# Extra products in TensorE's gaps between the output projection and the first expert

## The chip, the cores and the metric

The kernel runs on one core of a Trainium2 chip. The metric is the device time of one execution in microseconds (us). Three runs of the kernel before took 1212.13, 1212.85 and 1215.75 us, a median of 1212.85.

## What is computed

One layer for 336 tokens (16 meta tokens, 256 of a prompt, 64 of eight samples) of 1024 channels. A retention branch and a convolution branch are merged, projected by `w_out` and normalised. Then each token goes through two of 16 experts. The part that matters here, cut from the reference:

```python
mixed = (sigmoid(m_r) * ret_out + sigmoid(m_c) * conv_out) @ w_out
x = _layernorm(alpha * x + mixed, ln1_g, ln1_b)
logits = (xt @ w_router).astype(float32) + b_router
probs = softmax(logits)                        # best group of four experts,
                                               # then the best two inside it
for e in range(16):
    he = silu(xt @ w_gate[e]) * (xt @ w_up[e])
    y = y + gates[:, e:e + 1] * (he @ w_down[e])
x = _layernorm(alpha * x + y, ln2_g, ln2_b)
```

## The kernel before

Each engine has its own program, written out by hand, and executes it in order. They wait for each other with semaphores. The tokens stand in three tiles t = 0, 1, 2 of 112. There are eight PSUM banks of 128 x 512 f32; each named result ("xt0", "log0") has a bank by a fixed turn, four banks for names of kind F and four for kind P. `room` waits until the result that had the bank before has been read out.

Weight products are split: a weight is rounded to a high part on ScalarE (`split_hi` line 1081, `hi_of` line 1265), the remainder is formed on VectorE (line 1086, line 1690), and TensorE multiplies in the format fp32r. The small products and the transposes are done in plain f32: the router, the positions, the gather by a matrix, and `prompt_state` of the retention stage (line 964).

The stage around the change goes like this.

- TensorE ends the output projection (`t_unit` with WOUT, line 1036). VectorE adds the residual and normalises each tile (lines 1627, 1609 to 1621), and increments `x1_ready` for each. The square root in it is ScalarE's (line 1246).
- For each tile t, TensorE waits for `x1_ready`, transposes the tile in eight pieces of 112 x 128 (`turn`, line 1053), and multiplies the transposed tile by the router's weights (`router`, line 1042). ScalarE copies the transposes out (line 1249); in its program the square root of tile t+1 stands behind the copies of tile t. The router's result log0 uses the bank that the last tile's output projection had, so its first product needs VectorE's line 1627 of tile 2. The transposes of tile 2 need log0's bank again, which VectorE reads out in line 1639, behind `x1_ready` of tile 2.
- VectorE then picks two experts per token in a chain of small operations (lines 1642 to 1663) and sets `chosen_ready`. TensorE counts the tokens ahead of each in its experts by products with a triangular matrix (lines 1059, 1062). VectorE reads this (line 1671) into `most_i`, on which all engines branch, then makes `picks` (line 1677) and the slots (line 1683).
- GpSimd scatters the tokens to `x_slots` in DRAM, six indirect DMAs (line 682), and once all have landed reads the tokens of expert 1 (`xg_tok`, line 686).
- The tokens of expert 0 don't take this way: TensorE gathers them with 24 products by `picks` (line 830). VectorE meanwhile scales y (line 1684), splits two weight units (line 1690), and then forms the low part of the gathered tokens (line 1695). Then the first expert starts (`expert`, line 800). Within it, after six of its twelve weight units, TensorE transposes the tokens of the next expert (`tokens`, line 768 and on), which it waits for by `xg_full`.

The weights come by SyncE's queue into eight slots, each released by VectorE's low part (line 505).

In the trace a plain f32 product shows as two MATMUL records and a transpose or an fp32r product as one; the names x and tab stand for x1 and for the tables, ident among them.

Of the kernel before, what the change touches and what calls it, by code (L numbers as in the profile page):

```python
# [158 lines left out]
def alone(eng, waits_met):  # L159

    eng.sem_inc(waits_met, 1)
# [13 lines left out]
def program(nc, x_prompt, x_sample, state_ret, state_conv, meta_tokens, w_in, b_in, w_ret_o, conv_w, conv_b,  # L175
# [10 lines left out]
    with ctx:  # L186
# [3 lines left out]
        def sb(name, shape, dt=f32):  # L190
            size = 4 * int(np.prod(shape[1:]))
            t = nc.alloc_sbuf_tensor_at(name, shape, dt, offset=base[0])
            base[0] += (size + 31) // 32 * 32
            high[0] = max(high[0], base[0])
            return t

        def sem(name):
            return ctx.enter_context(nc.semaphore(name))


        tab = sb("tab", [128, TBW])
# [123 lines left out]
        bank = [ctx.enter_context(nc.psum_tensor(f"bank{i}", [128, 512], f32)) for i in range(8)]  # L325
        ident = tab[:, TB["ident"][0]:TB["ident"][1]]
# [22 lines left out]
        CONV = Stage(GATE2, ["Fc0", "Fc1", "Fc2", "Fc3"], 2)  # L349
# [30 lines left out]
        evac = [sem(f"evac{i}") for i in range(8)]  # L380
# [51 lines left out]
        def T_view(t, slot):  # L432
            return t[:, slot, :].rearrange("p (k n) -> p k n", k=4)
# [286 lines left out]
        def _(pe):  # L720
# [24 lines left out]
            def t_unit(stage, half, parts, finals, it, wh, wl, xh, xl):  # L745

                for t in range(NT):
                    name = finals[t]
                    if half == 0:
                        room(stage, name, it)  # L750
                    out = bank[stage.bank[name]][0:TT, :]
                    mms = []
                    for k in range(4):
                        kk = 4 * half + k
                        first, last = half == 0 and k == 0, half == 1 and k == 3
                        xs = slice(t * TT, (t + 1) * TT)
                        mms += [(out, xh[:, kk, xs], wh[:, k, :], first, False), (out, xh[:, kk, xs], wl[:, k, :], False, False),
                                (out, xl[:, kk, xs], wh[:, k, :], False, last)]
                    group(stage, name, it, mms)
# [8 lines left out]
            def gathered_path():  # L768
                def tokens(stage, names, q, it, value):

                    pe.wait_ge(xg_full[q], value)
                    for j, name in enumerate(names):
                        b = bank[stage.bank[name]]
                        turn(stage, name, it, [(b[:, i * CAP:(i + 1) * CAP], xg_tok[:, q, (4 * j + i) * 128:(4 * j + i + 1) * 128], CAP) for i in range(4)])

                def half(stage, v, it, wit, name, kh, xh, xl):

                    pe.wait_ge(mlo_ready, U_PAIR.idx(v, wit) + (1 + MLEAD))
                    if kh == 0:
                        room(stage, name, it)  # L780
                    out = bank[stage.bank[name]][0:CAP, :]
                    wh, wl = T_view(mhi, v % MH), T_view(mlo, v % MH)
                    mms = []
                    for k in range(4):
                        kk = 4 * kh + k
                        mms += [(out, xh[:, kk, :], wh[:, k, :], kk == 0, False), (out, xh[:, kk, :], wl[:, k, :], False, False),
                                (out, xl[:, kk, :], wh[:, k, :], False, kk == KT - 1)]
                    group(stage, name, it, mms)

                def h_turn(stage, p, j, it):  # L790

                    pe.wait_ge(evac[stage.bank[f"u{p}{j}"]], stage.used(f"u{p}{j}", it) + 1)
                    alone(pe, waits_met)
                    b = bank[stage.bank[f"ht{p}{j}"]]
                    turn(stage, f"ht{p}{j}", it, [(b[:, i * CAP:(i + 1) * CAP], h_tok[:, (4 * j + i) * 128:(4 * j + i + 1) * 128], CAP) for i in range(4)])

                def evacuated(stage, name, it):
                    pe.wait_ge(evac[stage.bank[name]], stage.used(name, it) + 1)

                def expert(stage, p, it, wit, following):  # L800
                    v = 12 * p
                    xh, xl = xg_hi[:, p], xg_lo[:, p]
                    if p:
                        for j in range(2):
                            evacuated(stage, f"xt0{j}", it)
                    for u, name in ((0, f"g{p}0"), (2, f"u{p}0")):
                        for kh in range(2):
                            half(stage, v + u + kh, it, wit, name, kh, xh, xl)
                    for kh in range(2):
                        half(stage, v + 4 + kh, it, wit, f"g{p}1", kh, xh, xl)  # L810
                    h_turn(stage, p, 0, it)
                    if following:
                        tokens(stage, (f"xt{p}0", f"xt{p}1"), 1 - p, it, wit * 16 + 16)
                    for kh in range(2):
                        half(stage, v + 6 + kh, it, wit, f"u{p}1", kh, xh, xl)
                    for kh in range(2):
                        evacuated(stage, f"ht{p}{kh}", it)
                        for n in range(2):
                            half(stage, v + 8 + 2 * kh + n, it, wit, f"d{p}{n}", kh, hT_hi, hT_lo)
                            if kh == 0 and n == 0:  # L820
                                h_turn(stage, p, 1, it)

                pe.wait_ge(picks_ready, NT)
                for j in range(2):
                    room(FIRST, f"xt{j}", 0)
                    b = bank[FIRST.bank[f"xt{j}"]]
                    for i in range(4):
                        ch = (4 * j + i) * 128
                        for t in range(NT):
                            last = pe.matmul(b[:, i * CAP:(i + 1) * CAP], x1[:, t, ch:ch + 128], picks[:, t, :], start=t == 0, stop=t == NT - 1)  # L830
                    last.then_inc(group_done, 1)
                for j in range(2):
                    evacuated(FIRST, f"xt{j}", 0)
                for it in range(NE // 2 - 1):
                    for p in range(2):
                        if p == 0:

                            pe.wait_ge(turned, it + 1)
                        expert(PAIR, p, it, it, True)
                pe.wait_ge(turned, NE // 2)  # L840
                expert(LAST, 0, 0, NE // 2 - 1, True)
                expert(LAST, 1, 0, NE // 2 - 1, False)
# [18 lines left out]
            for t in (1, 2, 0):  # L861
# [4 lines left out]
                for j in range(2):  # L866
                    n = f"xt{2 * t + j}"
# [5 lines left out]
            for h in range(H):  # L873
# [61 lines left out]
                for t in (2, 1, 0):  # L935
# [5 lines left out]
                    if t == 0:  # L941
# [5 lines left out]
                        for r in range(2):  # L947
                            for p in range(2):
                                for c in range(4):
                                    i = pe.matmul(bank[HEAD.bank[name]][32 * c:32 * c + QC, :], qdiag[:, p, c + 4 * r, :], st[:, c + 4 * r, p, :],  # L950
                                                  start=False, stop=(r == 1 and p == 1), skip_group_check=True)
# [80 lines left out]
            for n in range(2):  # L1032
                for half in range(2):
                    pe.wait_ge(mlo_done, half + 1)
                    split_ready(U_WOUT, 2 * n + half, 0)
                    t_unit(WOUT, half, None, [f"w{n}{t}" for t in range(NT)], 0, T_view(hi, half), T_view(lo, half), m_hi, m_lo)
            def router(t):
                for n in (2 * t, 2 * t + 1):
                    pe.wait_ge(evac[X1T.bank[f"xt{n}"]], X1T.used(f"xt{n}") + 1)
                room(X1T, f"log{t}", 0)  # L1040
                out = bank[X1T.bank[f"log{t}"]]
                group(X1T, f"log{t}", 0, [(out[0:TT, 0:NE], x1T_f[:, k, t * TT:(t + 1) * TT], wr_sb[:, k, :], k == 0, k == KT - 1) for k in range(KT)])
# [5 lines left out]
            for t in range(NT):  # L1048
                pe.wait_ge(x1_ready, t + 1)
                for j in range(2):  # L1050
                    n = f"xt{2 * t + j}"
                    b = bank[X1T.bank[n]]
                    turn(X1T, n, 0, [(b[:, i * TT:(i + 1) * TT], x1[:, t, (4 * j + i) * 128:(4 * j + i + 1) * 128], TT) for i in range(4)])
                router(t)

            pe.wait_ge(chosen_ready, 1)
            room(X1T, "pos", 0)
# [2 lines left out]
            for i in range(NT):  # L1060
                n = NT - i
                last = pe.matmul(out[0:TT, (i + 1) * NE:(NT + 1) * NE].rearrange("p (t e) -> p t e", t=n), ones_t,
                                 gt[:, 7, i, :].unsqueeze(1).to_broadcast([TT, n, NE]), start=False, stop=True, skip_group_check=True)
            last.then_inc(group_done, 1)
            pe.wait_ge(most_ready, 1)
            with pe.If(pe.value_load(most_i[0:1, 0:1], min_val=0, max_val=T) <= CAP):
                gathered_path()
# [756 lines left out]
```

## Time and profile before

| | |
|---|---|
| median of three runs | 1212.85 us |
| the profiled execution's own time | 1213.8 us |
| its span, first to last instruction | 1212.0 us |
| TensorE busy | 1120.5 us (92%) |
| VectorE busy | 955.2 us (79%) |
| ScalarE busy | 637.9 us (53%) |
| mean granted TensorE clock | 0.965 |

A granted clock of 1.00 is 2.4 GHz, 0.50 is 1.2 GHz. The span runs through three long parts: retention and convolution up to about 548 us, the stage described above from there to about 608 us, and the experts up to about 1170 us, with the last normalisation behind. A time such as 573.34 is counted from the span's start. A row of a timeline gives the start, the length of the whole merged group, the engine, the line, the operation, out<-in and the count; in brackets stands the idle time ahead of it and what ended it.

### The profile page before, as it was taken

The page shows a single profiled execution, that of the slowest core. Times are in us where ns is not written, and L with a number is a line of the kernel's source. Part 1 is how long each engine was busy: PE and PEld are TensorE (multiplying, and loading weights), DVE is VectorE, ACT ScalarE, POOL GpSimd, SP SyncE. Part 2 cuts the span into 40 slices and gives each one's busy share as a digit, 9 for nine tenths or more (in the row PEclk, how much of TensorE's full clock was granted, in tenths as well). Part 3 has the DMA queues.
Part 4 walks back from the last instruction along what each step waited for, and adds up shares of the span by engine and source line. Part 5 has one row for each costly group of instructions (what it writes and reads, how often), then busy time and mean ns, then how long its engine had stood idle before and what let it go on. Part 6 is the DMA issues. An engine that isn't in the chain of part 4 may idle for free.

```text
span 1212.0 us, 15132 instructions
## 1 busy us (share of the span) xinstructions
PE 1120.5 (92%) x5829; PEld 873.8 (72%) x5829; DVE 955.2 (79%) x1021; ACT 637.9 (53%) x582; POOL 127.3 (10%) x219
## 2 busy tenths in 40 slices
PE   4999999999999999997799999999999999999960
PEld 4986986987798699985667676767766676776640
DVE  3598898889789885556568888888888888888846
ACT  2432433244243236431267777777777777777730
POOL 3120220220212030000210000000000000000012
PEclk9999999999999999998599999999999999999985
DMA  9663874785486395453399999999999999999924
GB/s 214 204 228 124 278 255 138 245 278 201 152 274 224 124 272 178 139 204 109 108 353 366 377 379 388 374 380 379 380 377 379 382 383 379 380 380 380 384 95 107
DMA packets 171323, 331.85 MB, mean 274 GB/s; under 512 B 8394, under 2 KB 45690, under 8 KB 171232
## 3 DMA queue, kind: packets, MB, share of 16 engines
q1 hardware_dynamic: 150624, 263.95, 62.1%
q0 software_dynamic: 20352, 66.41, 16.6%
q8 instruction: 49, 0.80, 0.3%
q10 hardware_dynamic: 272, 0.47, 0.2%
q14 instruction: 26, 0.21, 0.1%
HBM read 294.88 MB, written 36.63 MB: 274 GB/s over the span
## 4 chain that ended last, share of the span: by engine, by line
PE 78%; DVE 11%; DMA 4%; ACT 3%; issue 2%; POOL 1%; SPq 0%; POOLq 0%; DVEq 0%; ACTq 0%
PE bank L724 74%; PE bank L765 3%; DVE lo L1086 3%; DVE cT L1391 2%; DMA x_in<-in_x_prompt_dram 1%; ACT hi L1081 1%; PE bank L975 1%; DVE st L1535 1%; DMA x_slots<-x,slot 1%; POOL x_slots L682 1%; DMA xg_tok<-x_slots 1%; DMA y_back<-y_slots,slot 1%; ACT hi L1225 1%; DVE o_tok L1497 0%; DVE stats L1489 0%
## 5 line engine op out<-in xcount | busy, mean ns | idle before, releaser
L1690 DVE TENSOR_TENSOR mlo<-mraw,mhi 128x2048 fp32r<-128x2048 f32 x192 | 439.4, 2289 | 78.8 <-ACT mhi L1265 75.5
L1265 ACT ACTIVATE mhi<-mraw 128x2048 fp32r<-128x2048 f32 x192 | 367.4, 1915 | 91.7 <-PE bank L724 85.0
L724 PE MATMUL bank<-mhi,xg_hi 128*96 128x512 f32 x512 | 203.0, 396 | 1.4 <-DVE xg_lo L1695 1.4
L724 PE MATMUL bank<-mhi,xg_lo 128*96 128x512 f32 x512 | 202.7, 396 | 0.0
L724 PE MATMUL bank<-mlo,xg_hi 128*96 128x512 f32 x512 | 201.5, 394 | 0.0
L1081 ACT ACTIVATE hi<-raw 128x2048 fp32r<-128x2048 f32 x47 | 89.9, 1914 | 195.0 <-PE bank L724 167.5
L1086 DVE TENSOR_TENSOR lo<-raw,hi 128x2048 fp32r<-128x2048 f32 x56 | 128.3, 2291 | 78.6 <-ACT hi L1081 43.5
L724 PE MATMUL bank<-xT_hi,hi 128*128 128x336 f32 x512 | 166.0, 324 | 3.1 <-DVE lo L1086 1.7
L724 PE MATMUL bank<-xT_hi,lo 128*128 128x336 f32 x512 | 163.9, 320 | 0.0
L724 PE MATMUL bank<-xT_lo,hi 128*128 128x336 f32 x512 | 163.8, 320 | 0.0
L1391 DVE SCALAR_TENSOR_TENSOR cT<-W,vec,cT 128x336 f32<-128x336 f32 x240 | 118.6, 563 | 0.0
L724 PEld LDWEIGHTS bank<-mhi,xg_hi 128*96 128x96 f32 x512 | 82.9, 162 | 36.2 <-issue 1.7
L724 PEld LDWEIGHTS bank<-mhi,xg_lo 128*96 128x96 f32 x512 | 82.9, 162 | 36.1
L724 PEld LDWEIGHTS bank<-mlo,xg_hi 128*96 128x96 f32 x512 | 83.2, 162 | 35.5
L724 PE MATMUL bank<-mhi,hT_hi 128*96 128x512 f32 x256 | 101.7, 397 | 0.0
L724 PEld LDWEIGHTS bank<-xT_hi,hi 128*128 128x128 f32 x512 | 98.7, 193 | 4.0 <-DVE lo L1086 2.0
L724 PE MATMUL bank<-mhi,hT_lo 128*96 128x512 f32 x256 | 100.8, 394 | 0.0
L724 PE MATMUL bank<-mlo,hT_hi 128*96 128x512 f32 x256 | 100.6, 393 | 0.0
L724 PEld LDWEIGHTS bank<-xT_lo,hi 128*128 128x128 f32 x512 | 98.7, 193 | 0.2
L724 PEld LDWEIGHTS bank<-xT_hi,lo 128*128 128x128 f32 x512 | 98.6, 193 | 0.0
L724 PE MATMUL bank<-hi,xT_lo 128*112 128x512 f32 x144 | 56.9, 395 | 0.0
L697 POOL DMA_DIRECT2D y_slots<-yo x14 | 7.1, 507 | 467.2 <-ACT yo L1294 467.2
(253 smaller groups left out, 1496.6 us busy)
## 6 DMA issues: line engine op xcount, KB each, us to landing
mraw<-in_w_gate_dram SPq DMA_DIRECT2D x64, 1024.0 KB, 11.4
mraw<-in_w_up_dram SPq DMA_DIRECT2D x64, 1024.0 KB, 11.3
mraw<-in_w_down_dram SPq DMA_DIRECT2D x64, 1024.0 KB, 12.0
raw<-in_w_in_dram SPq DMA_DIRECT2D x40, 1024.0 KB, 6.7
st<-in_state_ret_dram POOLq DMA_DIRECT2D x32, 512.0 KB, 5.0
out_dram<-st POOLq DMA_DIRECT2D x32, 512.0 KB, 4.5
raw<-in_w_ret_o_dram SPq DMA_DIRECT2D x8, 1024.0 KB, 5.4
x_slots<-zeros POOLq DMA_DIRECT2D x12, 512.0 KB, 4.2
```

The lines of the kernel that those rows point to most:

```text
L682: pool.indirect_dma_start(x_slots, bass.IndirectOffsetOnAxis(slot[:, k, t:t + 1], 0), x1[:, t, :], None).then_inc(scattered, 16)
L697: pool.dma_start(y_slots[ds((it * 2 + p) * CAP, CAP), :], yo[:, p, :]).then_inc(yo_stored, 16)
L724: i = pe.matmul(out, a, b, start=s, stop=e)
L765: i = pe.transpose(out, in_, ident[0:n, 0:n])
L975: i = pe.matmul(bank[HEAD.bank[f"st{b}{p}"]][:, :], a[rows, b // 4, cols], v[rows, :], start=k == 0, stop=k == 2)
L1081: act.activation(dst[:, hslot, :], src[:, slot, :], ACT.Copy).then_inc(ready, 1)
L1086: dve.tensor_tensor(l[:, u % RH, :], src[:, u % R, :], h[:, u % RH, :].bitcast(f32), ALU.subtract).then_inc(lready, 1)
L1225: act.activation(hi[:, slot, :], raw[:, slot, :], ACT.Copy).then_inc(hi_ready, 1)
L1265: act.activation(mhi[:, v % MH, :], mraw[:, v % MR, :], ACT.Copy).then_inc(mhi_ready, 1)
L1391: ins = dve.scalar_tensor_tensor(out, src, tap, out, ALU.mult, ALU.add)
L1535: dve.scalar_tensor_tensor(st[:, s, p, :], st[:, s, p, :], hs[:, HGAM:HGAM + 1], b[:, :], ALU.mult, ALU.add).then_inc(e, 1)
L1690: dve.tensor_tensor(mlo[:, v % MH, :], mraw[:, v % MR, :], mhi[:, v % MH, :].bitcast(f32), ALU.subtract).then_inc(mlo_ready, 1)
```

## The change

A function `keep_warm(n)` issues n plain f32 products of the 128 x 128 identity by 512 columns of the tables, all into the bank of the convolution's last result c3, which nobody reads again before a later product overwrites it. It is called eight times in TensorE's program: behind the transposes of tile 0, 1 and 2 with 12, 1 and 1; behind the router's products of these tiles with 3, 7 and 12; behind the products for the positions with 3; and behind the gather of the first expert's tokens with 2. No other engine's program is changed, and no semaphore is incremented by the products.

```diff
@@ -829,6 +829,7 @@
                     last.then_inc(group_done, 1)
+                keep_warm(2)
                 for j in range(2):
                     evacuated(FIRST, f"xt{j}", 0)
@@ -1034,7 +1035,14 @@
+            def keep_warm(n):
+
+                pe.wait_ge(evac[CONV.bank["c3"]], CONV.used("c3", 1) + 1)
+                for _ in range(n):
+                    pe.matmul(bank[CONV.bank["c3"]][:, :], ident, tab[:, 128:640], start=True, stop=True)
+
             def router(t):
+                keep_warm((12, 1, 1)[t])
                 for n in (2 * t, 2 * t + 1):
                     pe.wait_ge(evac[X1T.bank[f"xt{n}"]], X1T.used(f"xt{n}") + 1)
@@ -1052,6 +1060,7 @@
                 router(t)
+                keep_warm((3, 7, 12)[t])
 
             pe.wait_ge(chosen_ready, 1)
@@ -1062,6 +1071,7 @@
             last.then_inc(group_done, 1)
+            keep_warm(3)
             pe.wait_ge(most_ready, 1)
```

## Rows read from the trace of the kernel before

**Rows 1.** The page: busy time of the engines; TensorE's granted clock in 40 slices.
```profile
PE 1120.5 (92%) x5829; PEld 873.8 (72%) x5829; DVE 955.2 (79%) x1021; ACT 637.9 (53%) x582; POOL 127.3 (10%) x219
...
PEclk9999999999999999998599999999999999999985
```

**Rows 2.** The chain of waits, 540 to 690 us: start, length, what.
```profile
578.64 0.10 ACT lnmv L1246
...
594.46 0.19 DVE most L1671
...
598.92 5.12 POOL x_slots L682
...
609.29 10.49 DMA x_slots<-x,slot
...
620.38 7.60 DMA xg_tok<-x_slots
```

**Rows 3.** Stretches: length, busy time by engine, TensorE's granted clock, DMA share, GB/s.
```profile
570.00:573.30 3.30, 0.00 (x0) 0.00 (x0) 3.13 (x5) 0.00 (x0) 0.00 (x0) 0.52 0.00 0
573.30:588.00 14.70, 12.72 (x64) 11.93 (x64) 5.44 (x11) 3.55 (x6) 0.55 (x16) 0.50 0.32 111
...
607.96:611.03 3.07, 3.07 (x8) 2.02 (x8) 2.15 (x1) 0.88 (x1) 2.67 (x2) 0.50 1.04 406
611.03:626.30 15.27, 15.27 (x69) 10.61 (x68) 10.47 (x7) 11.28 (x7) 1.51 (x2) 1.00 0.99 340
```

**Rows 4.** TensorE's timeline, 566 to 629 us.
```profile
566.35 1.22 PE L765 MATMUL bank<-tab,x 112*128 112x112 f32 x8 [0.86 <-issue]
573.34 3.14 PE L724 MATMUL bank<-wr_sb,x1T_f 128*112 128x16 f32 x16 [5.78 <-DVE x L1627]
576.32 1.73 PE L765 MATMUL bank<-tab,x 112*128 112x112 f32 x8
...
584.81 3.14 PE L724 MATMUL bank<-wr_sb,x1T_f 128*112 128x16 f32 x16 [0.68 <-issue]
592.68 0.61 PE L1059 MATMUL bank<-gt,tab 112*112 112x48 f32 x2 [4.73 <-DVE gt L1663]
...
595.99 10.53 PE L830 MATMUL bank<-picks,x 112*128 112x96 f32 x48 [1.64 <-DVE picks L1677]
607.96 0.71 PE L724 MATMUL bank<-mhi,xg_hi 128*96 128x512 f32 x1 [1.44 <-DVE xg_lo L1695]
...
628.11 0.85 PE L765 MATMUL bank<-tab,xg_tok 96*128 96x96 f32 x8 [1.50 <-DMA xg_tok<-x_slots]
```

**Rows 5.** TensorE's plain f32 products in the retention stage: groups by form, timeline.
```profile
L724 PE MATMUL bank<-v_tok,kdp 112*128 112x512 f32 x48 | 22.0, 595 | 0.0
...
82.78 0.55 PE L724 MATMUL bank<-qr,kr 128*112 128x112 f32 x4
...
100.94 2.75 PE L724 MATMUL bank<-v_tok,kdp 112*128 112x512 f32 x6
```

**Rows 6.** VectorE's timeline, 572 to 608 us.
```profile
572.51 0.68 DVE L1627 SCALAR_TENSOR_TENSOR x<-x_tok,bank 112x512 f32<-112x512 f32 x1
...
578.76 0.81 DVE L1614 TENSOR_SCALAR x<-x,lnmv 112x1024 f32<-112x1024 f32 x1 [3.41 <-ACT lnmv L1246]
...
582.13 0.26 DVE L1639 TENSOR_TENSOR gt<-bank,br_bc 112x16 f32<-112x16 f32 x2
...
603.07 0.55 DVE L1695 TENSOR_TENSOR xg_lo<-bank,xg_hi 128x384 fp32r<-128x384 f32 x1
607.14 0.56 DVE L1695 TENSOR_TENSOR xg_lo<-bank,xg_hi 128x384 fp32r<-128x384 f32 x1 [3.52 <-ACT xg_hi L1269]
```

**Rows 7.** ScalarE's timeline: copies of the transposes of tile 0, square root of tile 2.
```profile
566.96 1.19 ACT L1249 ACTIVATE x1T_f<-bank 128x448 f32<-128x448 f32 x2 [4.08 <-PE bank L765]
...
578.53 0.19 ACT L1246 ACTIVATE lnmv<-lnmv 112x1 f32<-112x1 f32 x1
```

## The prediction

> **What bounds the kernel now.** I read the page first. TensorE is busy 92% of the span, and its clock is full except in slices 19 and 20 and in the last two [rows 1]. A slice is 30.3 us, so the low clock lies within 545 to 606 us and a little beyond: the stage between the output projection and the experts. The chain of waits shows what sets the time there. It is no engine at its peak but a relay: normalisation, transposes, router, choice of experts, positions, then scatter and reload of tokens by DMA [rows 2]. From the first expert on TensorE works without a gap, so a shift at its start or at its one late token read is a shift of the end. The reader is to see two paths in the rows. One leads through the gather to the first expert's start at 607.96 [rows 4]. The other leads from the positions, read at 594.46, over the six scatters and the reload, which ends at 627.98 [rows 2]; TensorE takes these tokens at 628.11 after a wait of 1.50 us [rows 4]. That wait decides: the second path is the late one, by 1.5 us. Last, the stretches give the clock. After 5.8 us without work it is at half, and stays there from 570 to 611 us [rows 3, 4]. What the change can give back is the price of this, and only where the work stands on a path.
>
> **The price of a product.** No row has the identity by 128x512 f32, but `prompt_state` has the same form with 112 instead of 128 rows: a plain f32 product of 512 columns, two records each. Six records take 2.75 us, and one record lasts 0.595 with its drain [rows 5], so records start (2.75 - 0.595) / 5 = 0.43 us apart and a product occupies TensorE for 0.86 us at full clock. Bounds: below, the fp32r product of 512 columns, one record every 15.27 / 69 = 0.22 us [rows 3]; above, half clock, 1.72. I take 0.86, since the row has the same type and width. The eight calls issue 12+3+1+7+1+12+3+2 = 41 products, 35.3 us of TensorE's time. The gaps that they are put into are 5.78, 0.68, 4.73, 1.64 and 1.44 us [rows 4], 14.3 us, and about the other three calls stands no more than 0.7 us each. TensorE executes in order, so what doesn't fit pushes what stands behind.
>
> The Trainium skill ("FP8 and Floating Point Precision", section TensorE Precision Notes) says that true FP32 takes four passes through the array; its page "TensorE: Matmul & The Clock Gate" gives about 0.216 us for one 512-column pass, so as an estimate by these pages a product takes 0.86 us. The trace agrees. The same page's table ("Why this matters for your kernels") asks that no idle gap over about 3 us stand between bursts, which speaks for the change; by it alone the sum would end at the second rival below.
>
> **The work at full clock.** The products begin while the clock is still full (it is at half only from 570 us [rows 3]), so I take full clock from here to the first expert. Half-clock rows are halved: the router's 16 records from 3.14 to 1.6 us, eight transposes from 1.73 to 1.0, positions from 1.7 to 0.9, gather from 10.53 to 5.3 [rows 4]. The nearest row at full clock is 0.55 us for four small f32 records [rows 5], 0.14 each with the drain, which would make the router 2.2 at most; the other end is 1.4.
>
> **Step by step, TensorE's program in the changed kernel.**
> - Transposes of tile 0 end at 567.5 as before [rows 4]. Twelve products, 10.4 us: to 577.9. The router's bank has been free since 573.2 [rows 6] and its input since 568.2 [rows 7], so the products, not the bank, are now what it waits for.
> - Router of tile 0 to 579.5, three products to 582.1. Only now come the transposes of tile 1, at 576.32 before [rows 4].
> - This hits another engine. ScalarE's square root of tile 2 stands behind its two copies of these transposes. From the start of transposes to the end of copies were 1.8 us at full clock (566.35 to 568.15) [rows 4, 7]; the root then starts at about 583.8 instead of 578.53, and VectorE's line 1614 at 584.0 instead of 578.76 [rows 6, 7]: 5.3 later. `x1_ready` of tile 2 comes at 587.4, log0 is read out at 587.6 (before: 582.3 [rows 6]).
> - TensorE meanwhile: one product to 584.0, router of tile 1 to 585.6, seven products to 591.6. It is 4.0 late for tile 2's transposes. Those to 592.6, one product to 593.5 (the copies end by then), router to 595.2. Before it ended at 587.95 [rows 4]: 7.2 later. The 20 products of this and the steps before cost 17.3 us, half hidden by gaps that were there.
> - Twelve products: to 605.5. VectorE's choice takes 4.7 us from the router's end [rows 4] and is done at 599.9, so 5.6 us of the products stand on the path. Positions to 606.4, read at 606.5 instead of 594.46 [rows 2]: **12.0 later**.
>
> **Path over the DMAs.** All behind the positions moves with it: slots, scatters, reload. The first weight splits move by the same, so the weight loads that the scatters compete with do so too. The tokens of expert 1 land at 628.0 + 12.0 = 640.0.
>
> **Path over the gather.** Three products to 609.0 (picks are ready at 607.8, 1.2 are visible), gather 5.3 to 614.3, two products to 616.0. VectorE scales y and splits two units first: its low parts start at 603.07 + 12.0 = 615.1, twice 0.55 [rows 6]: 616.2, which hides the two products. First expert at 616.4, 8.4 later. It starts at full clock: eight records took 3.07 where eight at full clock take 1.8 [rows 3], and the turn-over was within the eighth; I take 1.4. So TensorE asks for the tokens of expert 1 at 626.6 + 8.4 - 1.4 = 633.6. It then waits 6.4 us.
>
> That wait is longer than the 5.8 after which the clock was at half before [rows 3, 4], so the clock falls during it, and the restart costs what the first expert's start cost: about 3 us at half speed, 1.5 us lost. Bounds: 0 and 2.
>
> **Sum:** 12.0 + 1.5 = 13.5 us behind 628.11, and nothing later gives it back, as TensorE has no wait there in which it could. Against the profiled execution's own time of 1213.8 us (span 1212.0) this is 1227.3. It lies 1 us above the median of 1212.85, so against the median: **1226.4**, I say 1226.5. Router and transposes each a third off would move the sum by 2 us, the scatters' traffic by 2 either way (units are released in part some 4 us sooner against the scatter than before, and one unit takes near 3 us at 380 GB/s). The case's own range is 1222 to 1231.
>
> **Rivals.**
> - *Tokens are not the late path.* If scatter and reload go faster because weight loads stop once the eight slots are full, then only TensorE's stream counts: 8.4 - 1.4 = 7.0. Result 1220. For it: 7.60 us for a reload of 0.4 MB shows queueing [rows 2]. Against: the weights' demand comes at the same time as before.
> - *The products cost less and fill the gaps only* (the other side, not slower). At one record of 0.43 each, the first twelve end at 572.7, before the bank is free; tile 2's normalisation is about as before, its router ends at 586.1 (1.9 sooner), twelve products take 5.2 and just cover the choice; the positions come 2.2 sooner. The expert starts 5.8 sooner, but the tokens only 2.2, so the wait of 6.5 us brings a half clock there, +1.5: about -0.7, 1212. At 0.22 each the positions come 4.0 sooner: 1213 - 4.0 + 1.5 = 1210.5. It decides from the price: below some 0.45 us a product the chain is not delayed. For it: the counts 12, 12 and 3 by 0.43 are 5.2, 5.2 and 1.3 against gaps of 5.78, 4.73 and 1.64. Against: every plain f32 product in the trace has two records, each at 0.43 for 512 columns.
> - *More contention or a clock that falls in the products' stretch.* Then the products cost up to 1.72: every us at half clock on the 30 us path up to the positions costs one more; two such spells make 1233 and more.
>
> **Chances.** Forecast 0.82 (1226.5), tokens early 0.06 (1220), cheap products 0.08 (1210.5 to 1212.5), still slower 0.04 (1233). The range 1220 to 1231 takes in the first and half of the second. What can be told from no change is 0.3%, 3.6 us: 1209.2 to 1216.5. The cheap case lies within it but for a quarter: faster 0.02, same 0.07, slower 0.91.
>
> **What would show it.** In the profile after: 82 records at `keep_warm`'s line, starts 0.43 us apart (right) or less (second rival). Full clock in all stretches from 553 to 633 us. VectorE's line 1614 of tile 2 at 584, the read of the positions (line 1671 of before) at 606.5, the first expert's product at 616.4, and a wait of about 6 us for `xg_tok` with half clock behind it. If the positions are late by 12 but the wait is under 3 us, the first rival holds. The prediction is wrong if the first router product starts before 577.

## The result: 1.0092 times the time of before

The changed kernel takes 1223.84 us (median of four runs, 1223.10 to 1226.15) against 1212.74 us for the kernel before (four runs). The ratio is 1.0092, with a 95% interval of 1.0073 to 1.0110, so 11.1 us slower (8.9 to 13.3). The forecast was 1226.5, in a range of 1220 to 1231.

TensorE is busier, its mean clock is higher (0.980 against 0.965), and the kernel is slower. The page, parts 1 and 2, answers to [rows 1]:

```profile
PE 1141.5 (93%) x5911; PEld 875.6 (72%) x5911; DVE 955.5 (78%) x1021; ACT 638.1 (52%) x582; POOL 128.2 (10%) x219
...
PEclk9999999999999999999989999999999999999985
```

The 82 new records are there (5911 against 5829), and the dip of the clock in slices 19 and 20 has become one dip in slice 21. TensorE's timeline shows where the time went. Line 1042 is the new product.

```profile
562.88 1.22 PE L765 MATMUL bank<-tab,x 112*128 112x112 f32 x8 [0.86 <-issue]
563.93 10.48 PE L1042 MATMUL bank<-tab 128*128 128x512 f32 x24
574.25 1.65 PE L724 MATMUL bank<-wr_sb,x1T_f 128*112 128x16 f32 x16
575.75 2.82 PE L1042 MATMUL bank<-tab 128*128 128x512 f32 x6
578.41 0.93 PE L765 MATMUL bank<-tab,x 112*128 112x112 f32 x8
...
581.64 6.25 PE L1042 MATMUL bank<-tab 128*128 128x512 f32 x14
587.73 0.93 PE L765 MATMUL bank<-tab,x 112*128 112x112 f32 x8
...
590.96 10.55 PE L1042 MATMUL bank<-tab 128*128 128x512 f32 x24
601.34 0.31 PE L1068 MATMUL bank<-gt,tab 112*112 112x48 f32 x2
...
612.19 0.44 PE L724 MATMUL bank<-mhi,xg_hi 128*96 128x512 f32 x1 [0.23 <-DVE xg_lo L1705]
...
635.19 1.51 PE L765 MATMUL bank<-tab,xg_tok 96*128 96x96 f32 x8 [5.78 <-DMA xg_tok<-x_slots]
```

Set beside [rows 4], the gaps are gone: no idle time stands between 563 and 610 us. But from the first router on, all work whose result is used comes later. The last twelve products start at 590.96 and end at 601.3, while VectorE's choice was ready at 595.8, so 5.5 us of them stand on the path. VectorE's timeline shows both delays, the square root's and the positions', against [rows 2, 6]:

```profile
580.10 0.81 DVE L1624 TENSOR_SCALAR x<-x,lnmv 112x1024 f32<-112x1024 f32 x1 [8.21 <-ACT lnmv L1256]
...
595.58 0.21 DVE L1673 TENSOR_TENSOR gt<-gt 112x48 f32<-112x48 f32 x1
...
602.32 0.17 DVE L1681 TENSOR_REDUCE most<-bank 112x1 f32<-112x16 f32 x1 [5.63 <-PE bank L1071]
```

**How to compare two executions here.** In this profile tile 0's transposes start at 562.88 us, 3.5 us earlier than in [rows 4], though nothing ahead of them was changed. Over all the profiles of this case, whose programs agree up to there, the start lies between 562.9 and 567.3. The two profiles are 2.0 us apart already at an early row of the retention stage (80.75 us in this profile, 82.78 in [rows 5]), so more than half of the shift is there long before the stage of the change; where it comes from is open. So the table counts from this start. "Late tokens" is when TensorE takes the second expert's tokens; "last output" is when ScalarE starts its last copy of an expert's result.

| kernel | positions read | late tokens | last output | timed against before, us (95%) |
|---|---|---|---|---|
| before | 28.1 | 61.8 | 603.6 | |
| changed | 39.4 | 72.3 | 615.9 | +11.1 (8.9 to 13.3) |
| e1, last twelve alone | 34.6 | 70.3 | 614.8 | +5.7 (3.0 to 8.3) |
| e2, 256 columns | 25.7 | 59.4 | 604.2 | -0.6 (-2.7 to 1.5) |
| e3, counts fitted | 27.5 | 61.7 | 605.6 | +1.5 (-0.4 to 3.4) |
| e4, changed + hold | 39.4 | 72.3 | 614.3 | +9.1 (5.8 to 12.3) |
| e6, first twelve alone | 30.6 | 64.1 | 606.0 | +1.8 (-0.7 to 4.4) |
| e7, without the 3 and the 7 | 37.6 | 70.2 | 614.8 | +9.6 (6.6 to 12.6) |
| e8, 256 columns + hold | 25.7 | 62.1 | 604.0 | -0.7 (-2.4 to 1.0) |
| e9, 256 columns + gather | 25.7 | 54.3 | 600.6 | -4.5 (-6.2 to -2.9) |
| e10, gather alone | 28.1 | 60.4 | 606.7 | +3.4 (1.7 to 5.2) |

For e9 and e10 "late tokens" is the start of the gather that replaces the wait. The last column is the ratio and its interval, less one, times the median of the kernel before (for the changed kernel the difference of the medians). The ratio can differ from the ratio of the two medians, most in e1: 1.0047 against 1.0063. One profiled execution can differ from the median by some 3 us, and the last output and the timed difference by more: in e1 the profile's last output is 11.2 us later, the time 5.7.

### The profile page after: what moved, and what is told of

It is laid out like the page before. It is cut to its first block, busy times and chain, and to the rows that moved or that the text cites. A ratio compares the mean times of both kernels' runs of the same rounds, so it can differ in the third digit from the quotient of the medians.

```text
span 1221.2 us, 15296 instructions
## 1 busy us (share of the span) xinstructions
PE 1141.5 (93%) x5911; PEld 875.6 (72%) x5911; DVE 955.5 (78%) x1021; ACT 638.1 (52%) x582; POOL 128.2 (10%) x219
## 4 chain that ended last, share of the span: by engine, by line
PE 81%; DVE 9%; DMA 3%; ACT 3%; issue 2%; POOL 1%; SPq 0%; POOLq 0%; DVEq 0%; ACTq 0%
PE bank L724 74%; PE bank L765 3%; DVE lo L1096 3%; PE bank L1042 3%; DVE cT L1401 2%; DMA x_in<-in_x_prompt_dram 1%; ACT hi L1091 1%; PE bank L976 1%; DVE st L1545 1%; POOL x_slots L682 1%; DMA x_slots<-x,slot 1%; DMA y_back<-y_slots,slot 1%; ACT hi L1235 1%; DMA xg_tok<-x_slots 1%; DVE o_tok L1507 0%
## 5 line engine op out<-in xcount | busy, mean ns | idle before, releaser
L1096 DVE TENSOR_TENSOR lo<-raw,hi 128x2048 fp32r<-128x2048 f32 x56 | 128.3, 2291 | 75.0 <-ACT hi L1091 41.6
L724 PEld LDWEIGHTS bank<-mhi,xg_hi 128*96 128x96 f32 x512 | 82.9, 162 | 35.7 <-DVE xg_lo L1705 1.0
## 6 DMA issues: line engine op xcount, KB each, us to landing
mraw<-in_w_up_dram SPq DMA_DIRECT2D x64, 1024.0 KB, 10.3
```

What stands on the lines that cost most here:

```text
L724: i = pe.matmul(out, a, b, start=s, stop=e)
L1096: dve.tensor_tensor(l[:, u % RH, :], src[:, u % R, :], h[:, u % RH, :].bitcast(f32), ALU.subtract).then_inc(lready, 1)
```

## The experiments

All are shown as edits of the changed kernel. Each was timed beside the kernel before on its own chip: e1 to e4 on one, e6 to e9 on a second, e10 on a third. No run is called e5.

### e1: the last twelve alone

```diff
-                keep_warm((12, 1, 1)[t])
+                keep_warm(0)
...
-                keep_warm((3, 7, 12)[t])
+                keep_warm((0, 0, 12)[t])
...
-            keep_warm(3)
...
-                keep_warm(2)
```

> Only the twelve products between the last router product and the products for the positions are left; the other 29 are gone. Theory (products are serial work on TensorE at 0.86 us each at full clock, and what does not fit its gap delays the positions): they start at about 587.9 us at half clock, two of them at 1.7 us until the clock rises, ten at 0.86, so they end at 600.0 against a choice of experts ready at 592.6; the positions are read at 600.8 instead of 594.5 (6.3 later), the gather runs at full clock, the first expert starts near 610.7, TensorE waits about 6 us for the tokens of the second expert and restarts at half clock: +6.3 + 1.5 = +7.8 us, 1220.5. Rival (the delay came from the square root behind tile 1's transposes, which this kernel leaves alone): within 1.5 us of before, 1212.7.

Measured: 1221.21 us, against 1213.54 for the kernel before on that chip, ratio 1.0047 (1.0025 to 1.0068). TensorE's timeline:

```profile
585.04 11.98 PE L1041 MATMUL bank<-tab 128*128 128x512 f32 x24
...
599.37 5.57 PE L830 MATMUL bank<-picks,x 112*128 112x96 f32 x48 [1.64 <-DVE picks L1685]
607.72 0.45 PE L724 MATMUL bank<-mhi,xg_hi 128*96 128x512 f32 x1 [2.78 <-DVE xg_lo L1703]
...
633.54 1.51 PE L765 MATMUL bank<-tab,xg_tok 96*128 96x96 f32 x8 [7.01 <-DMA xg_tok<-x_slots]
```

Twelve products take 11.98 us, as the clock is low at their start, and the positions come 6.4 us later than before (theory 6.3). The first expert starts only 2.8 us later (44.4 against 41.6 after tile 0's transposes), but what it has regained of the position delay is lost in a wait of 7.01 us for the tokens. In this profile the way over the DMAs was also 2.0 us longer, 35.7 us from the positions to the tokens against 33.7. The rival (within 1.5 us of before) is out, as the measured interval starts at 3.0 us; it holds the theory's +7.8.

### e2: products of half the width

```diff
-                    pe.matmul(bank[CONV.bank["c3"]][:, :], ident, tab[:, 128:640], start=True, stop=True)
+                    pe.matmul(bank[CONV.bank["c3"]][:, 0:256], ident, tab[:, 128:384], start=True, stop=True)
```

> The same 41 products, each with 256 columns instead of 512, so half the price: 0.43 us. Theory (price times count decides): the first twelve end before log0's bank is free, the last twelve (5.2 us) about cover the choice of experts (4.7), the positions come some 2 us sooner than in the kernel before, the wait for the second expert's tokens grows to about 6 us and costs a restart at half clock of 1.5: 1212.0 us, within 1.5 of before. Rival (instruction count or the calls as such delay the chain): near 1223.8, the time with 512 columns.

Measured: 1214.18 us, ratio 0.9995 (0.9978 to 1.0012). The same 82 records at half the width cost the whole 11 us less, so the delay comes from the products' length, not from their number. TensorE's timeline:

```profile
566.22 5.36 PE L1042 MATMUL bank<-tab 128*128 128x256 f32 x24
572.17 1.72 PE L724 MATMUL bank<-wr_sb,x1T_f 128*112 128x16 f32 x16 [0.59 <-DVE x L1637]
...
584.67 5.43 PE L1042 MATMUL bank<-tab 128*128 128x256 f32 x24
589.93 0.31 PE L1068 MATMUL bank<-gt,tab 112*112 112x48 f32 x2
...
600.88 0.45 PE L724 MATMUL bank<-mhi,xg_hi 128*96 128x512 f32 x1 [1.98 <-DVE xg_lo L1705]
...
624.61 1.51 PE L765 MATMUL bank<-tab,xg_tok 96*128 96x96 f32 x8 [6.52 <-DMA xg_tok<-x_slots]
```

Twelve take 5.36 us and end before log0's bank is free; the router waits for VectorE again. The positions come 2.4 us sooner, the first expert 5.9 us, the late tokens 2.3 us, and the last output 0.6 us later than before: from the tokens to the last output it takes 544.8 us instead of 541.8. The time itself can't be told from before.

### e3: full width, counts fitted to the gaps

```diff
-                keep_warm((12, 1, 1)[t])
+                keep_warm((6, 0, 0)[t])
...
-                keep_warm((3, 7, 12)[t])
+                keep_warm((0, 2, 5)[t])
...
-            keep_warm(3)
+            keep_warm(1)
...
-                keep_warm(2)
+                keep_warm(1)
```

> Full width, but the counts fitted to the gaps at 0.86 us a product: 6 behind tile 0's transposes, 2 behind tile 1's router, 5 behind tile 2's router, 1 behind the positions, 1 behind the gather, 15 in all. Theory: no step is delayed and all small products run at full clock; tile 2's normalisation about 2 us sooner, its router ends at 583.9 instead of 588.0, positions read at 589.5 instead of 594.5, that is 5.0 sooner; the first expert starts 8 us sooner but the tokens of the second only 5, so TensorE waits about 7 us for them and restarts at half clock (+1.5): 1209.3 us. Rival (products in the gaps cost as such, or the clock does not matter in this stage): 1212.7 or more.

Measured: 1215.16 us, ratio 1.0012 (0.9997 to 1.0028), where 1209.3 was expected. The theory failed on its premise that the clock would stay full. Stretches of TensorE: length, busy time, granted clock, DMA share, GB/s:

```profile
566.30:571.60 5.30, 5.30 (x14) 1.00 0.46 177
571.60:575.60 4.00, 2.54 (x25) 1.00 0.00 0
575.60:582.00 6.40, 6.36 (x21) 0.52 0.26 85
...
586.00:591.70 5.70, 5.70 (x10) 0.70 0.02 6
```

No gap in 571.6 to 575.6 was longer than 0.9 us. TensorE had the router's and the transposes' small records in it, busy 2.54 of 4.00 us, and the clock fell all the same. The two products behind tile 1's router then took 3.76 us at half clock, longer than their gap, and the five behind tile 2's took 6.23. So the positions gained 0.6 us instead of 5.0. The stretches are of one execution; the mean clock of all twelve timed ones was 0.970 to 0.975, against 0.975 to 0.979 in e2.

### e4: the changed kernel, and products ahead of the token wait

```diff
                     h_turn(stage, p, 0, it)
+                    if it == 0 and p == 0 and stage is PAIR:
+                        keep_warm(6)
                     if following:
```

> The changed kernel with six more products, 5.2 us, put ahead of TensorE's wait for the second expert's tokens, which took 5.78 us in its profile. Theory (the wait lets the clock fall, and the restart at half clock costs 1.5 us): full clock through this stretch, 1.6 us less than the changed kernel, 1222.2. Rival (the clock falls anyway, or the time behind it is bound by the weights' DMAs, so that the restart cost nothing): 1223.8, no difference.

Measured: 1223.59 us, ratio 1.0075 (1.0048 to 1.0101). The interval overlaps the changed kernel's, so the time alone decides nothing. The stretches behind the token wait show the mechanism. The changed kernel's, columns as in [rows 3]:

```profile
629.50:635.00 5.50, 0.00 (x0) 0.00 (x0) 3.91 (x3) 2.45 (x3) 0.00 (x0) 0.71 1.04 346
635.19:638.64 3.45, 3.45 (x14) 2.70 (x15) 1.12 (x2) 0.98 (x2) 0.00 (x0) 0.50 1.05 388
638.64:645.90 7.26, 7.26 (x33) 5.08 (x32) 3.42 (x3) 3.84 (x2) 0.00 (x0) 1.00 0.72 262
```

And this kernel's:

```profile
631.50:638.50 7.00, 6.40 (x25) 3.14 (x24) 4.24 (x3) 3.19 (x5) 0.00 (x0) 1.00 1.04 356
638.50:646.00 7.50, 7.50 (x34) 5.26 (x33) 3.81 (x4) 4.29 (x4) 0.00 (x0) 1.00 1.04 383
```

The tokens are taken at 72.3 us in both. The last output comes 1.6 us sooner with the hold (614.3 against 615.9): the restart at half clock did cost 1.6 us in that execution, as expected. The other profiles bear this out. Where TensorE's wait for the tokens was 1.5 us or less (before, e4, e6, e8), the last output follows them by 541.8 to 542.0 us; where it was 5.49 us or more (the changed kernel, e1, e2, e3, e7), by 543.6 to 544.8.

### e6 and e7: the first twelve alone, and the changed kernel without the middle ones

```diff
# e6: the other calls are gone
-                keep_warm((12, 1, 1)[t])
+                keep_warm((12, 0, 0)[t])
# e7
-                keep_warm((3, 7, 12)[t])
+                keep_warm((0, 0, 12)[t])
```

> Only the twelve products behind tile 0's transposes. Theory (they overrun the 5.8 us gap by 4.6, the router at full clock gives back 1.5, tile 1's transposes come 3 us late, and with them the square root that ScalarE takes behind their copies): tile 2's normalisation (line 1624 here) starts 14.6 us after the first transpose of tile 0 instead of 12.4, and all behind it is 2.2 us later: 1215.0 us. Rival (the overrun is hidden, as tile 2's normalisation is VectorE's): no difference, 1212.8.

Measured: 1214.34 us, ratio 1.0015 (0.9994 to 1.0036). The time doesn't exclude the rival, the profile does: VectorE's timeline has tile 2's normalisation 14.6 us after tile 0's transposes (566.84), as worked out, with ScalarE's square root as the releaser, and the positions are 2.5 us late.

```profile
581.43 0.81 DVE L1622 TENSOR_SCALAR x<-x,lnmv 112x1024 f32<-112x1024 f32 x1 [5.59 <-ACT lnmv L1254]
```

> The changed kernel without the 3 products behind tile 0's router and the 7 behind tile 1's; 31 products are left. Theory: tile 1's transposes 2.6 us sooner, and with them tile 2's normalisation, which now decides when tile 2's transposes start (18.2 us after tile 0's instead of 24.9); positions read 32.6 us after tile 0's transposes instead of 39.4, so 6.8 us less than the changed kernel: 1217.0. Rival one (every product costs its 0.86 us on the path): 8.6 less, 1215.2. Rival two (only the last twelve cost): 1223.8.

Measured: 1223.20 us, ratio 1.0079 (1.0054 to 1.0104), near the changed kernel; its profile has the positions 1.9 us sooner, not 6.8. Ten products of 8.6 us are gone, and what is gained, 1.5 us between the two ratios, is not clear of the noise. TensorE's timeline and, below it, its stretches show why:

```profile
581.70 1.73 PE L765 MATMUL bank<-tab,x 112*128 112x112 f32 x8 [2.11 <-DVE gt L1649]
583.21 1.94 PE L1042 MATMUL bank<-tab 128*128 128x512 f32 x2
584.95 3.03 PE L724 MATMUL bank<-wr_sb,x1T_f 128*112 128x16 f32 x16
587.82 12.25 PE L1042 MATMUL bank<-tab 128*128 128x512 f32 x24
```

```profile
579.60:581.70 2.10, 0.01 (x1) 0.84 0.00 0
581.70:588.00 6.30, 6.30 (x27) 0.50 0.94 315
588.00:591.00 3.00, 3.00 (x4) 0.50 0.13 44
```

The transposes start 18.4 us after tile 0's (theory 18.2), so the order of waits was right. But the clock is at half from 581 to about 591 us. Transposes, one product, router and twelve products together take 4.7 us more than in the changed kernel (1.73, 1.94, 3.03, 12.25, in sum 18.95, against 0.93, 1.04, 1.72, 10.55, in sum 14.24). In these two profiles the middle products nearly pay for themselves, and what they hold the clock for is above all the last twelve products, which nobody needs. Rivals one and two of this run both miss the positions; by time, rival two can't be told from what happened.

### e8: products of 256 columns, and a hold

The edit of e2 and that of e4 with `keep_warm(15)`.

> The kernel with products of 256 columns, and 15 more of them, 6.5 us, ahead of TensorE's wait for the second expert's tokens. Theory (in the 256-column kernel the positions come 2.4 us sooner, counted from tile 0's transposes, but the restart at half clock behind the token wait eats it): the restart goes, 2 us less than the kernel before: 1211 us. Rival (what is behind the wait is not bound by TensorE's clock): like the 256-column kernel, no difference from before.

Measured: 1212.20 us, ratio 0.9994 (0.9980 to 1.0008). Inconclusive: the last output follows the tokens by 542.0 us, as without a restart, but in this profile the tokens themselves are 2.6 us later than in e2, though the positions are not. The way over the DMAs took 36.3 us from the positions on, against 33.7 in e2 and before, 32.9 in the changed kernel and 32.6 in e7. That spread is larger than the effect looked for. The clock differed too, ahead of the added products, where the program is that of e2. In e2 the first expert's records have full length from the start (0.39 us behind the first); here, after the same idle time of 1.98 us, its first seven ran at half clock:

```profile
601.64 0.71 PE L724 MATMUL bank<-mhi,xg_hi 128*96 128x512 f32 x1 [1.98 <-DVE xg_lo L1707]
602.15 0.63 PE L724 MATMUL bank<-mlo,xg_hi 128*96 128x512 f32 x1
```

### e9 and e10: the second expert's tokens gathered by TensorE

Cut marks stand for loop lines, the declarations of `picks1` and `rank1`, and in e9 the edit of e2. The scatter and the reload by DMA still run, but TensorE no longer waits for them here; GpSimd does.

```diff
# e9: e2, and on GpSimd, behind the reload
+                pool.wait_ge(xg_full[1], 16)
...
# TensorE, in tokens()
+                    if stage is PAIR and it == 0 and q == 1:
+                        pe.wait_ge(picks_ready, 2 * NT)
+                        for j, name in enumerate(names):
+                            room(stage, name, it)
...
+                                for t in range(NT):
+                                    last = pe.matmul(b[:, i * CAP:(i + 1) * CAP], x1[:, t, ch:ch + 128], picks1[:, t, :], start=t == 0, stop=t == NT - 1)
+                            last.then_inc(group_done, 1)
+                        return
...
# VectorE
+            dve.tensor_copy(rank1[:, :], b[0:TT, 1:NT * NE:NE])
...
+                for t in range(NT):
+                    dve.tensor_scalar(picks1[:, t, :], row[:, :], rank1[:, t:t + 1], gt[:, 7, t, 1:2], ALU.is_equal, ALU.mult).then_inc(picks_ready, 1)
# e10: the same without keep_warm and its calls
```

> The kernel with products of 256 columns, and the second expert's tokens are gathered by TensorE with 24 more products (5.5 us at full clock) as the first's are, instead of awaited from the scatter and reload by DMA; VectorE makes a second set of picks. Theory (the late DMA path ate what the earlier first expert brings): TensorE asks for them 52.4 us after tile 0's transposes start, goes on to weights at 58 instead of 62.4 in the kernel before: 4.4 us less, 1208.5. Rival (the weights' DMAs then become the bound): no difference from before, 1212.8.

Measured: 1209.08 us against 1213.22, ratio 0.9963 (0.9949 to 0.9976), 4.5 us less than before (2.9 to 6.2). This version beats both kernels, and by time the 4.4 of the theory is met. Its profile shows less: the gather starts 54.3 us after tile 0's transposes, not 52.4, as the first expert's first eight records ran at half clock, and the last output is 2.9 us sooner than before. This execution was the slowest of the twelve (1212.55 us). TensorE's timeline:

```profile
603.03 0.62 PE L727 MATMUL bank<-mhi,xg_hi 128*96 128x512 f32 x1 [1.92 <-DVE xg_lo L1720]
...
621.32 0.49 PE L768 MATMUL bank<-tab,h_tok 96*128 96x96 f32 x4
621.65 5.52 PE L782 MATMUL bank<-picks,x 112*128 112x96 f32 x48
```

> The kernel before, without any of the unread products, but with the second expert's tokens gathered by TensorE. It tells whether the gain of the gather kernel (1209.1 us) is the gather's alone. Theory (the two only pay together): the first expert starts as in the kernel before, TensorE is ready for the second expert's tokens 1.5 us ahead of where the DMA landed, and spends 5.5 us on the gather instead of 1.5 of wait and 0.85 of transposes: 3 us slower than before, 1216 us. Rival (the gather alone brings the gain, since the scatter path is off the end): 1209.

Measured: 1214.63 us against 1211.46, ratio 1.0028 (1.0014 to 1.0043), 3.4 us slower. So the gather alone loses, the half-width products alone gain nothing (e2), and both together gain 4.5. The difference between e9 and e10, 7.9 us by the two ratios (an estimate from their intervals: 5.5 to 10.3), is what the unread products of half the width are worth once TensorE no longer waits for the DMA path.

## Why the prediction was right

Its steps, counted from tile 0's transposes (566.35 in [rows 4]):

- **Price of a product.** 0.86 us was taken; 24 records take 10.48 us with the last one's drain, of 0.59, so (10.48 - 0.59) / 23 = 0.43 a record. Right, and e2 shows that the length is the cause.
- **The router waits for the products, not for its bank.** It starts at 11.4 us (predicted 11.5). The prediction calls itself wrong if the router starts before 577 us, and it starts at 574.25. Taken literally, that sign speaks against it; it forgot that this stage starts at a different time in each execution. Counted from tile 0's transposes, as everything here, 577 stands for 10.65 us, and the router's 11.37 lies behind it.
- **The square root behind tile 1's transposes.** Tile 2's normalisation starts at 17.2 us (predicted 17.6), and the wait for ScalarE's root has grown from 3.41 to 8.21 us. e6 shows this step alone. The prediction says that 20 products had been passed up to the end of tile 2's router, 17.3 us; it is 24, or 20.6 us. The sum doesn't use the figure: its steps contain all 24. The router's end, 7.2 us later by the prediction, came 6.6 later.
- **Positions.** 11.3 us later (predicted 12.0). The small products at full clock were a little cheaper than taken: transposes 0.77 instead of 1.0 up to the next start, positions 0.7 instead of 0.9.
- **The DMA path decides.** TensorE waits 5.78 us for the tokens (predicted 6.4), which are 10.6 us later, not 12.0. Of the missing 1.4, 0.7 is the positions' and 0.8 the DMAs', which took 32.9 us instead of 33.7. This way took 32.6 to 36.3 us over the profiles, so that this one came so near is in part luck; the prediction allowed 2 us either way.
- **The restart.** 1.5 us was taken; tokens to last output took 543.6 instead of 541.8, so 1.8, and e4 takes 1.6 of it back. In e1, e2 and e7 it was 2.7 to 2.9, above the prediction's upper bound of 2.

The sum in the profiles is 10.6 + 1.8 = 12.4 us, where 13.5 was predicted, and 11.1 by the medians. So the mechanism was right step by step, and the size a little too large: 13.5 lies just above the measured interval of 8.9 to 13.3.

**What was too simple.** The claim that the stretch runs at full clock held for the changed kernel, in which TensorE idled nowhere for more than 0.23 us between 563 and 629 us. But when the clock falls was not understood: e3 and e7 show it falling with gaps no longer than 0.9 us and of 2.1 us, where small records stood around them. The prediction also treated each product as a pure cost once its gap is full. e7 suggests that the middle ten were nearly free. The second rival's forecast for cheaper products, -0.7 us, is what e2 measured (-0.6), and its steps are met too (positions 2.4 us sooner for 2.2, first expert 5.9 for 5.8, a wait of 6.52 for 6.5), but for the restart, 2.9 instead of 1.5; the interval of the time, -2.7 to 1.5, would hold either.

## What to carry to other kernels

An engine that works in order has no spare time, only gaps: filler longer than its gap delays all behind it, and here also an operation of another engine that stood behind a copy of the delayed result. Before filling gaps to gain clock, find which path ends last. Here it was a DMA path, and the clock paid only after TensorE's wait for it had been taken away (e9), while taking it away alone lost (e10). Size filler by its measured length at the clock it will find, and compare two executions from a common event, not from the span's start.

## What the runs showed of the hardware

**When the clock falls.** In e3 the clock fell to half (0.52 from 575.6 to 582.0 us) after a stretch in which TensorE was busy 2.54 of 4.00 us with records of 16 and 112 columns and had no gap over 0.9 us. In e2, with 256-column products between the same small records, TensorE had gaps of 0.59 us and less up to the gather, and its twelve last products ran at the full rate (5.43 us for 24 records). Whether the longer gaps or the missing products made the difference is not separated. "TensorE: Matmul & The Clock Gate" of the Trainium skill says in its Part 4 that a transpose "doesn't count as PE-busy the same way" for the clock gate. No run here tests this, as transposes and the router's small records stand in the same stretch of e3. The rule that the prediction takes from the same page, no idle gap over about 3 us, was kept in e3, and the clock fell all the same.

**One program, two clocks.** e2 and e8 have the same program up to the first expert and both idle 1.98 us ahead of it. e2 went on at full clock, e8 at half for about 3 us (601.64 to 604.7 at 0.50). So what one profile shows of the clock need not hold for the next execution, and this goes for e3 and e7 too.

**The price of a restart.** Behind the long waits for the tokens TensorE ran at half clock for about 3.5 us (the changed kernel, e3), 5.6 (e1, e7) and 6.1 (e2). The way from the tokens to the last output was longer than the 541.8 us of before by 1.8 and 2.0, by 2.7 and 2.8, and by 2.9: about half of the spell each time. How long the spell lasts differs between the profiles, and what sets it is open.
